# A two-layer decoder trunk on one core: one-hots in two instructions, gate stores in pieces, other places for the second matrix's inputs, another gather schedule

## The reference

```python
q = (hc @ wq).reshape(t, PEER_HEADS, 2, D_KEY_HALF)
s = jnp.einsum("thpk,pnk->thpn", q, sk)
s1, i1 = lax.top_k(s[:, :, 0], PEER_TOPK)             # 16 of 128 keys, for each of 8 heads
s2, i2 = lax.top_k(s[:, :, 1], PEER_TOPK)
cand = (s1[..., :, None] + s2[..., None, :]).reshape(t, PEER_HEADS, PEER_TOPK * PEER_TOPK)
best, j = lax.top_k(cand, PEER_TOPK)
e = take(i1, j // PEER_TOPK) * N_KEYS + take(i2, j % PEER_TOPK)      # expert numbers
gate = jax.nn.softmax(best, axis=-1)
act = gelu(jnp.einsum("thkd,td->thk", u_tab[e], hc))
return jnp.einsum("thk,thkd->td", gate * act, v_tab[e])
```

## Time and profile before

| | |
|---|---|
| median of three runs | 3143.73 us (3141.48 to 3150.63) |
| the profiled run | 3141.54 us, its span 3139.8 us |
| TensorE busy | 2904.3 us, 93% |
| VectorE busy | 2430.9 us, 77% |
| GpSimd busy | 1424.9 us, 45% |
| ScalarE busy | 1207.3 us, 38% |
| mean granted TensorE clock | 0.975 |
| bytes moved | 849.74 MB, mean 271 GB/s |

### The profile page before, as it was taken

One profiled execution on the slowest core, in us unless ns is written; L12 is line 12 of the kernel. 1 busy time (PEld: TensorE's weight loads), 2 busy tenths in 40 slices (PEclk: granted clock), 3 DMA queues, 4 the chain that ended last, 5 costly groups with the idle time before them and its releaser, 6 DMA issues.

```text
span 3139.8 us, 50852 instructions
## 1 busy us (share of the span) xinstructions
PE 2904.3 (93%) x15754; PEld 2554.2 (81%) x15754; DVE 2430.9 (77%) x4532; ACT 1207.3 (38%) x1590; POOL 1424.9 (45%) x878
## 2 busy tenths in 40 slices
PE   5888999999998899999899899999999989999997
PEld 3657999989888788888777689989888878888885
DVE  7965679999995688888765307799999937888887
ACT  2333333345553333333333324333555523333332
POOL 2623367776667122222324244777766651222221
PEclk8999999999999999999999899999999989999998
DMA  6336567779898899999935124777788898999996
GB/s 240 134 128 221 199 206 240 242 263 349 308 350 321 301 353 350 355 356 352 351 122 174 66 100 138 229 251 239 277 328 328 310 348 308 352 353 351 357 347 232
DMA packets 352434, 849.74 MB, mean 271 GB/s; under 512 B 30048, under 2 KB 194016, under 8 KB 350176
## 3 DMA queue, kind: packets, MB, share of 16 engines
q1 hardware_dynamic: 239888, 479.53, 44.5%
q0 software_dynamic: 73728, 268.47, 23.6%
q10 hardware_dynamic: 38736, 100.84, 8.1%
HBM read 741.76 MB, written 106.95 MB: 270 GB/s over the span
## 4 chain that ended last, share of the span: by engine, by line
PE 54%; DVE 21%; issue 11%; POOL 7%; DMA 4%; ACT 1%; SPq 0%; POOLq 0%; DVEq 0%; ACTq 0%
PE bank L1418 11%; PE bank L1419 11%; PE bank L1420 11%; POOL w_lo L407 6%; DVE oh_c L995 5%; DVE oh_j L999 5%; PE bank L1360 4%; PE bank L1362 4%; PE bank L1361 4%; DVE rows L1160 2%; PE bank L1260 2%; PE bank L1262 2%; PE bank L1261 2%; DVE oh_i L996 2%; DMA x<-u_rows,u_idx 1%
## 5 line engine op out<-in xcount | busy, mean ns | idle before, releaser
L407 POOL TENSOR_TENSOR w_lo<-w_raw,w_hi 128x1024 fp32r<-128x1024 f32 x338 | 838.6, 2481 | 694.1 <-ACT w_hi L517 692.2
L517 ACT ACTIVATE w_hi<-w_raw 128x1024 fp32r<-128x1024 f32 x594 | 629.1, 1059 | 1346.3 <-PE bank L1420 668.6
L1360 PE MATMUL bank<-h_hi,w_hi 128*128 128x384 f32 x2048 | 702.7, 343 | 42.5 <-POOL w_lo L407 29.8
L1362 PE MATMUL bank<-h_lo,w_hi 128*128 128x384 f32 x2048 | 688.9, 336 | 0.0
L1361 PE MATMUL bank<-h_hi,w_lo 128*128 128x384 f32 x2048 | 688.3, 336 | 0.0
L461 POOL DMA_INDIRECT shared<-stream,v_idx x256 | 246.8, 964 | 830.9 <-DVE rows L1069 746.6
L1418 PE MATMUL bank<-w_hi,h_hi 128*128 128x512 f32 x1536 | 600.7, 391 | 16.6 <-ACT h_hi L642 14.3
L1419 PE MATMUL bank<-w_hi,h_lo 128*128 128x512 f32 x1536 | 600.0, 391 | 0.0
L1420 PE MATMUL bank<-w_lo,h_hi 128*128 128x512 f32 x1536 | 599.8, 390 | 0.0
L1039 DVE TENSOR_TENSOR w_lo<-w_raw,w_hi 128x1024 fp32r<-128x1024 f32 x256 | 313.7, 1226 | 199.9 <-ACT w_hi L517 199.0
L1360 PEld LDWEIGHTS bank<-h_hi,w_hi 128*128 128x128 f32 x2048 | 387.1, 189 | 58.9 <-issue 55.9
(11 more groups left out here) (193 smaller groups left out, 3584.6 us busy)
## 6 DMA issues: line engine op xcount, KB each, us to landing
w_raw<-stream SPq DMA_DIRECT2D x600, 512.0 KB
act_dram<-act_words ACTq DMA_DIRECT2D x256, 192.0 KB
gate_dram<-shared ACTq DMA_DIRECT2D x12, 4096.0 KB, 16.1
act_words<-act_dram SPq DMA_DIRECT2D x256, 192.0 KB
shared<-gate_dram SPq DMA_DIRECT2D x128, 384.0 KB
oh_j<-mod_rows SPq DMA_DIRECT2D x60, 512.0 KB, 4.7
oh_i<-mod_rows SPq DMA_DIRECT2D x20, 512.0 KB, 5.4
shared<-mod_rows SPq DMA_DIRECT2D x16, 512.0 KB, 14.0
```

The source lines that it names most:

```text
L407: nc.gpsimd.tensor_tensor(lo_of(grp, s), w_raw[:, s, :], hi_of(grp, s).bitcast(F32), ALU.subtract).then_inc(S["lo_ready"], 1)
L517: nc.scalar.activation(hi_of(grp, s), w_raw[:, s, :], ACT.Copy).then_inc(S["hi_ready"], 1)
L1360: MM(o, hi, h_hi[:, k, P:T], start=(k == 0), stop=False)
L1362: ins = MM(o, hi, h_lo[:, k, P:T], start=False, stop=(k == KC - 1))
```

## The change

It does the following, in both layers:

- The one-hots are written by two instructions instead of five. The two compares become one over oh_i and oh_c, which now lie in one tile `oh_ic`; the three products become one over oh_j. Keys and gate parts are stored group by group for that.
- EARLY is 30 instead of 36: block 1 has one set of six dots (behind the candidate sums), blocks 2 and 3 have two (behind L878 and behind the candidate sums), none stands behind the copies. Groups 0 to 5 get one dot more each.
- Gathers of block 1 stand behind tiles 3 to 8 of its 16; those of blocks 2 and 3 behind tiles 0 to 5 and 7 to 11.
- A half's gates are stored in eight pieces of 512 KB, issued among the next half's tiles (two, two, one, one, one, one); those of the last half at once.
- The second matrix's activations have a place of their own (`act_v`), and the first four are loaded before the last two first-matrix tiles' weights. The products' parts lie in columns of h_hi and h_lo that the first matrix doesn't read (`product`), so tile 0's product is made before the last first-matrix tile ends. The Gelu of all 128 dots stands in front of it.
- V_RING is 8 instead of 4, and `axpy` starts with tile 0, so that none is left behind the last tile.
- The loops over blocks on VectorE and over groups on ScalarE are unrolled.

```diff
-V_RING = 4
+V_RING = 8
+GATE_PIECES = 8
+GATE_STORED = 16 * GATE_PIECES
-EARLY = 2 * DB * EARLY_SET
+EARLY = (2 * DB - 1) * EARLY_SET
-    return EARLY + g + (g + 1) // 2
+    return EARLY + g + (g + 1) // 2 + min(g, EARLY_SET)
...
+        oh_ic = sb("oh_ic", [P, 3, PAIR, NK, 2], BF16)
+        oh_i, oh_c = oh_ic[:, 0:2, :, :, :], oh_ic[:, 2, :, :, :]
+        gate_p = key_words[:, 0:3 * DT].rearrange("p (g w t) -> p g w t", w=3, t=GROUP)
+        keys_t = key_words[:, 3 * DT:5 * DT].rearrange("p (g w t) -> p g w t", w=2, t=GROUP)
...
-        prod = part(2048, 2, DT)
+        prod = part(1536, 2, DT)
+        act_v = part(2304, RING, DT)
-        v_row_ring = part(8192, V_RING, D)
+        v_row_ring = part(4096, V_RING, D)
+        def product(h, s):
+            return h[:, DB * (s % 2):DB * (s % 2) + DB, 0:P]
...
                 for s in range(2):
+                    load(first - 1, s)
+                for r in range(2):
+                    sp.wait_ge(g_st[r], GATE_STORED * ((l + 1) * DB + 1))
+                for s in range(RING):
+                    sp.wait_ge(act_st[s], 16 * (l * EXPERT_TILES // RING + 1))
+                    load_products(0, s)
+                for s in range(2, RING):
+                    load(first - 1, s)
+                for s in range(RING):
                     load(first, s)
...
-                        end = 2 * (b - 1) * EARLY_SET + min(max(r - 1, 0), EARLY_SET) + (
-                            EARLY_SET if r == TILES_PER_BLOCK - 1 else max(r - 10, 0))
+                        if b == 1:
+                            end = min(max(r - 2, 0), EARLY_SET)
+                        else:
+                            end = (2 * b - 3) * EARLY_SET + min(r + 1, EARLY_SET) + (
+                                min(r - 6, EARLY_SET) if 7 <= r < 11 else EARLY_SET if r >= 11 else 0)
...
+                pieces = [range(0, 2), range(2, 4), range(4, 5), range(5, 6), range(6, 7), range(7, 8), (), ()]
+                for n in range(2 * DB):
+                    half = n % 2
+                    act.wait_ge(g_st[half], GATE_STORED * (l * DB + n // 2 + 1))
+                    for g in range(HALF // GROUP):
+                        expert_step(at + (n * (HALF // GROUP) + g) // RING, g % RING)
+                        if n:
+                            for piece in pieces[g]:
+                                store_gates(n - 1, piece)
...
                 def first_prod_hi():
-                    act.wait_ge(S["tile_done"], BASE[f"v{l}"])
+                    act.wait_ge(S["dot"], (l + 1) * SLOTS)
+                    nc.scalar.activation(dots[:], dots[:], ACT.Gelu).then_inc(S["dot_act"], 1)
                     prod_hi(0, 0, True)
...
                 def early_dots(b, half):
+                    done = 2 * b - 3 + half
+                    for n in range(max(done, 0) * EARLY_SET, (done + 1) * EARLY_SET):
+                        dot(n)
...
                     then_top(ins)
+                    if not fetched:
+                        early_dots(b, 0)
                     for hp in range(2 * HEADS):
                         ins = V.max(top_v[:, hp, 8:16], work2[:, hp, :])
...
-                    V.tensor_tensor(oh_c[:], keys, of_group(j_t, g), ALU.is_equal).then_inc(S["oh_cmp"], 1)
-                    V.tensor_tensor(oh_i[:, s, :, :, :], keys, of_group(i_t, g), ALU.is_equal)
+                    V.tensor_tensor(oh_ic[:, s:3:2 - s, :, :, :], keys, of_group(keys_t, g), ALU.is_equal
+                                    ).then_inc(S["oh_cmp"], 1)
                     dve.wait_ge(S["oh_cmp"], groups + g + 1)
-                    for w in range(3):
-                        ins = V.tensor_tensor(oh_j[:, s, w, :, :, :], oh_c[:], of_group(gate_p[:, w, :], g), ALU.mult)
-                    ins.then_inc(S["oh_ready"], 1)
+                    V.tensor_tensor(oh_j[:, s, :, :, :, :], oh_c.unsqueeze(1).to_broadcast([P, 3, PAIR, NK, 2]),
+                                    of_group(gate_p, g), ALU.mult).then_inc(S["oh_ready"], 1)
...
+                for s in range(2 * RING):
+                    two_ahead(s // RING, s % RING, 2 * RING)
+                    axpy(s)
```

192 lines of the change are left out of this document (84 added, 108 removed).

## The result

The changed kernel takes 3191.35 us (median of four, 3176.4 to 3197.6), the kernel before 3142.6 in the same session: 1.0136 times as long, 95% interval 1.0108 to 1.0164. That is slower, as the forecast leaned, but 38 us above the forecast of 3153 and 9 above the upper end of its range. The four times lie 21 us apart, and the profiled execution is the shortest (3176.4).

The account below looks back on a forecast made before the run. The prediction took TensorE, busy 93% of the span, as the bound, with four places above their matmul floors. Its terms summed to +6.6 us in layer 0 and +5.0 in layer 1: 3141.5+11.6=3153 us, range 3090 to 3182.

Parts of the forecast that it names:

- block 1: Second pick block of each layer: six dots instead of twelve, last gather one tile later, +0.2 us.
- blocks 2 and 3: Later pick blocks: VectorE waits for rows gathered later, 87.0 us per block against 73.2; +13.5, +13.4 and +13.5, +12.4.
- behind the third transposes: From there to the first one-hot matmul: no dots stand in front of w_lo any more, -4.7 and -5.1 us.
- groups: One-hot groups: TensorE waits for sets from group 3 on, 6.25 us per group, 294.2 us per layer; +7.6 and +8.3.
- last twelve tiles: End of the first matrix: gates stored in eight pieces leave gathers more turns, -3.5 and -8 us.
- joint to the third tile: Last first-matrix matmul to third second-matrix tile: first product and its load no longer wait, -10 us in each layer.
- third to ninth tile: Second-matrix tiles just behind the joint: the forecast had no term for them, 0.
- behind the last product: Before the transposes back: sums start at tile 0, so only copies of about 2 and 0.3 us remain; -9.9, -6.3.
- Rival B: Pick blocks: VectorE does not wait for rows, blocks stay at 71 to 73 us; 3091 to 3097 us, chance 0.15.
- the lead: One-hot groups: VectorE two sets ahead of TensorE gives 5.62 us per group, one ahead 6.25; forecast gone at group 3.
- rival C: Joint: the last dot, held up by product loads and gathers, gates the second matrix's start; 3184 us, chance 0.13.
- Rival D: One-hots: strided or repeated operands lose the bf16 rate, +2.7 us a set; 3280 us, chance 0.04.

Follow-up runs that it names:

- after_again: The changed kernel run and profiled once more, unedited: 3194.3 us, ratio 1.0149 to the kernel before.
- onehots: The kernel before with only the one-hots in two instructions: 3136.1 us, ratio 0.9975.
- picks_whole: picks_back with each half's gates stored by one issue, at once, as before the change: 3108.3 us, ratio 0.9881.
- picks_back: The changed kernel with the old gather rule and old dot places in the pick blocks, 36 early dots: 3085.3 us, ratio 0.9817.
- pieces_alone: The kernel before with only the gates stored in eight pieces, in the change's places: 3124.5 us, ratio 0.9943.
- group1: The changed kernel, but loads of products 4 to 7 wait only for their own tiles' stores: 3178.1 us, ratio 1.0117.

## Why the prediction was wrong

Working by its own steps, against after_again (span 3194.1, 54.3 above the one before), layer 0 and layer 1, in us:

| step | predicted | measured |
|---|---|---|
| block 1 | +0.2, +0.2 | +4.7, +4.5 |
| blocks 2 and 3 | +26.9, +25.9 | +28.0, +26.7 |
| behind the third transposes | -4.7, -5.1 | -1.2, -1.6 |
| groups | +7.6, +8.3 | +7.5, -0.1 |
| last twelve tiles | -3.5, -8 | +5.5, +5.7 |
| joint to the third tile | -10, -10 | -11.7, -11.5 |
| third to ninth tile | 0, 0 | +7.1, +9.2 |
| behind the last product | -9.9, -6.3 | -10.0, -6.5 |
| rest of the second matrix, end | 0 | -2.0 in all |

- **Pick blocks 2 and 3: right,** mechanism and size. The predicted 87.0 us per block is 86.6 to 88.9, with 33.5 us of waits for rows in two blocks. Rival B is refuted. The two halves of the step were each off by 2 us: the last dot of block 2 ended 57.7 us behind the transposes, not 55.7, and the tail was 29.0 us, not 31.3, so that the good total is partly luck. **Block 1 is off by 4.4 us a layer:** nothing made up for it there, and the tail, from the first candidate maximum at 470.05 to 504.13, is 34.1 us where the kernel before has 32.6 with gathers in it. So there the picks without gathers bought VectorE nothing; in blocks 2 and 3, where TensorE starves beside them, the tail is 29.0 to 30.7. I had taken block 0's tail for block 1, and that was 2.8 us too short; the sixth dot was 0.45 us later than I had it (first profile; after_again has another microsecond that I have not traced).
- **Groups: right in what happens,** the lead gone at group 3, 6.21 us after. The 294.2 us forecast for both layers, from the first group's start to the last one's, are 294.1 and 292.7 (295.7 and 294.2 with the last group's matmuls). Two things were wrong beside it. The baseline of layer 1 was read one tile short (285.9 for 292.8), so that +8.3 had to be about +1.4. And the lead is not lost for good: in one of two profiles a layer regained it. The price of the two-instruction form, nothing, is about right (onehots -8 us by its ratio, with an interval that takes in none); that of the pieces here, nothing, is wrong. I put the pieces' worth at the last twelve tiles, and it lies in the pace (picks_whole against picks_back 13.4 and 8.5 us in the profiles, 23 us by the medians, 18 with each taken against its own kernel before), where the new gather schedule kept it from showing.
- **Last twelve tiles: the step that failed,** by 9.0 and 13.7 us. Two terms of it were wrong. The gates in eight pieces were to give 3.5 and 8 us back, since the late row behind the 4 MB store would go. Alone they cost 0.7 and 0.3 us (pieces_alone): the sentence "Only the last store of a layer still goes out at once" gave the place and no price, and the eight issues in a row hold ScalarE's queue for 8.76 us, so that a stall of 3.4 to 6.9 us stands where one of 5.63 and 4.42 stood. And the loads of products ahead of the weights of tiles 126 and 127 were in the sum at nothing; I had seen them, as 1.6 MB that push towards rival C. They make those weights arrive 14.67 us after their issue and bring a second stall of 3.5 to 5.4 us in each layer, which the kernel before doesn't have. For layer 1, 7 of the 13.7 us are the misread row again: its 15.8 us of loss were 8.8. The number of matmuls in the row (340, where twelve tiles are 288) would have told it.
- **Third to ninth tile: not in the sum,** 16.3 us. The step took away the product loads' wait for the last four tiles' stores and did not ask where it went. That wait was put at nothing, and with it the step failed a second time. It stood four tiles on, and group1, which takes it away there, has the six tiles at 24.5 and 25.1 us for 24.5 before: it is nearly all of it.
- **Joint and end: right,** -39.7 us where the steps give -36.2. That no matmul at the joint would be at the lower clock level held up to tile 4. Rival C did not come in its form, as the last dot was at 1036.45, 12 us ahead of the last first-matrix matmul. Its place and price (3184) were nearest, which is luck as far as the price goes: the joint's gain is given back on both sides of it, by loads and waits and not by the last dot.
- **Behind the third transposes:** the two sets of dots are gone, but TensorE, which starved at the block's end, ran the five tiles at a granted clock of 0.89 (after_again, layer 0; 0.94 before): its matmuls take 23.9 us there for the 21.9 of the step, and it is idle for 1.5.
- **Rival D is refuted:** the product of 128x3072 takes 1.76 us, under 3.

Predicted -3.5-8 for the tail and 0 for the six tiles, measured +27.5 for both: 39 of the 43 us by which the sum missed the profiled 54.3. The rest cancels: block 1, the blocks and the stretch behind the transposes took 18 us more than the steps say, and the groups, joint and end 14 less. Of these 14, 7 are the misread row of layer 1, which made the groups' term too high and the tail's too low by that much; with it put right the tail and the six tiles miss by 32 us. What would have been needed was one look at each queue past the moved instructions, ScalarE's and SyncE's, as was done for GpSimd's.

## What to carry to other kernels

A wait that is moved is not removed: follow it to the next instruction that needs the same event (here four tiles on), and price each load that is moved forward by what then stands behind it on its queue (here the next weights). Measure a part alone before it gets the blame: the burst of eight issues had the longest row and cost 0.3 to 1.6 us. Where two engines run in lock, a few late transfers can fix the pace for all the rest, so judge a schedule by whether it keeps the lead, and look at more than one execution. And count the instructions in a window before building on its length.
